# The value products of a GLA and a differential attention as three rounded passes in place of plain float32 products

## The reference

```
# GLA, per head; computed here as one causal 256x256 score matrix a head
attn = where(causal, q_dec @ k_inv.T, 0)
o = attn @ v + (carried state part)        # the value product
o = rms_norm(o, head_gain) * silu(r)
# differential attention, per head
p = softmax(q @ k.T + alibi bias), two of them
a = p[0] - lam * p[1]
o = a @ v                                  # the value product
o = rms_norm(o, head_gain) * (1 - lambda_init)
```

## Time and profile before

| | us |
|---|---|
| median of 3 runs | 2195.97 (2195.87 to 2196.18) |
| span of the profiled execution | 2193.8 |
| time around the span (median less span) | 2.2 |
| PE busy | 2188.1 (100% of the span) |
| DVE busy | 1242.7 (57%) |
| ACT busy | 1058.2 (48%) |
| mean granted TensorE clock | 1.000 of full |

### The profile page before, as it was taken

The page is one execution under the profiler, slowest core; times in us unless marked ns, Lnnn a source line. Parts: engine busy times, 40 slices in busy tenths (PEclk is TensorE's granted clock), DMA queues, the critical chain, the costliest instruction groups (busy, mean ns, idle before and its releaser), DMA issues.

```text
span 2193.8 us, 27239 instructions
## 1 busy us (share of the span) xinstructions
PE 2188.1 (100%) x9720; PEld 1808.9 (82%) x9720; DVE 1242.7 (57%) x1460; ACT 1058.2 (48%) x1428; POOL 283.0 (13%) x563
## 2 busy tenths in 40 slices
PE   9999999999999999999999999999999999999999
PEld 7888788888888888888888888888888888888887
DVE  5665566655555555555566676665555555555443
ACT  6666455444444444444456665554444444444333
POOL 3210334100000000001125333341000000000000
PEclk9999999999999999999999999999999999999999
DMA  8765667666666666666667666676666666666664
GB/s 264 210 189 176 189 202 218 203 215 203 203 202 213 201 202 206 200 205 203 201 202 217 196 207 202 204 223 210 199 207 200 215 200 203 205 210 194 195 193 163
DMA packets 252675, 447.01 MB, mean 204 GB/s; under 512 B 27665, under 2 KB 41969, under 8 KB 252593
## 3 DMA queue, kind: packets, MB, share of 16 engines
q1 hardware_dynamic: 236176, 428.79, 62.2%
q0 software_dynamic: 16240, 17.07, 2.7%
q10 hardware_dynamic: 176, 0.07, 0.0%
HBM read 414.37 MB, written 2.10 MB: 190 GB/s over the span
## 4 chain that ended last, share of the span: by engine, by line
PE 100%; DVE 0%; ACT 0%; issue 0%; POOL 0%; DVEq 0%; ACTq 0%; POOLq 0%
PE acc L641 32%; PE acc L639 32%; PE acc L640 32%; PE acc L651 1%; PE acc L656 0%; PE side L884 0%; PE tps L678 0%; PE side L727 0%; PE side L703 0%; PE side L762 0%; PE side L882 0%; PE side L898 0%; PE side L899 0%; PE side L900 0%; PE side L782 0%; PE side L780 0%
## 5 line engine op out<-in xcount | busy, mean ns | idle before, releaser
L1311 DVE TENSOR_TENSOR w_lo<-raw,w_hi 128x1024 fp32r<-128x1024 f32 x784 | 954.8, 1222 | 835.6 <-ACT w_hi L945 831.3
L945 ACT ACTIVATE w_hi<-raw 128x1024 fp32r<-128x1024 f32 x784 | 827.8, 1059 | 1002.9 <-PE acc L641 994.0
L639 PE MATMUL acc<-w_hi,xT 128*128 128x512 f32 x2016 | 787.6, 391 | 0.0
L641 PE MATMUL acc<-w_hi,xT 128*128 128x512 f32 x2016 | 784.4, 389 | 0.0
L640 PE MATMUL acc<-w_lo,xT 128*128 128x512 f32 x2016 | 784.4, 389 | 0.0
L639 PEld LDWEIGHTS acc<-w_hi,xT 128*128 128x128 f32 x2016 | 378.4, 188 | 79.0 <-issue 0.7
L640 PEld LDWEIGHTS acc<-w_lo,xT 128*128 128x128 f32 x2016 | 378.4, 188 | 78.9 <-issue 0.7
L641 PEld LDWEIGHTS acc<-w_hi,xT 128*128 128x128 f32 x2016 | 378.4, 188 | 78.9
L639 PE MATMUL acc<-w_hi,hT 128*128 128x512 f32 x700 | 272.3, 389 | 0.0
L640 PE MATMUL acc<-w_lo,hT 128*128 128x512 f32 x700 | 272.3, 389 | 0.0
L641 PE MATMUL acc<-w_hi,hT 128*128 128x512 f32 x700 | 272.3, 389 | 0.0
(11 more groups left out here) (204 smaller groups left out, 1372.2 us busy)
## 6 DMA issues: line engine op xcount, KB each, us to landing
raw<-in_ffn_w_in SPq DMA_DIRECT2D x352, 512.0 KB, 3.8
raw<-in_ffn_w_out SPq DMA_DIRECT2D x176, 512.0 KB, 4.7
raw<-in_gla_w_in SPq DMA_DIRECT2D x96, 512.0 KB, 4.3
raw<-in_w_kv SPq DMA_DIRECT2D x64, 512.0 KB, 4.6
raw<-in_gla_w_out SPq DMA_DIRECT2D x32, 512.0 KB, 4.9
raw<-in_diff_w_q SPq DMA_DIRECT2D x32, 512.0 KB, 4.6
raw<-in_diff_w_out SPq DMA_DIRECT2D x32, 512.0 KB, 4.9
tok<-scratch SPq DMA_DIRECT2D x352, 32.0 KB, 2.9
```

Source lines behind the costliest of these rows:

```text
L639: nc.tensor.matmul(acc[p][tb][:, :], hi, w_hi[:, slot, j, :], start=(kt + j == 0), stop=False)
L641: last = nc.tensor.matmul(acc[p][tb][:, :], lo, w_hi[:, slot, j, :], start=False, stop=(kt + j == n_kt - 1))
L945: nc.scalar.activation(w_hi[:, slot, :, :], raw[:, slot, :, :], ACT.Copy).then_inc(hi_done, 1)
L1311: nc.vector.tensor_tensor(w_lo[:, slot, :, :], raw[:, slot, :, :], w_hi[:, slot, :, :].bitcast(F32), ALU.subtract).then_inc(lo_done, 1)
```

## The change

Both value products are computed from operands that are split into a rounded high part and the rest, and each product is three float32r passes (high by high, high by low, low by high). For that:

- PE: `three` issues the passes. A GLA head has 9 matmuls of 512 columns in place of 3, a pair of differential heads 18 of 256 columns in place of 6.
- Values: ACT writes the rounded copy at the same place as before (`v_out`), and DVE then makes the low part from PSUM (`v_low_out`). `evacuated`, on which PE waits, is now raised by DVE.
- GLA scores: ACT rounds them (`scores_high`, (b, 3) of blocks 5 to 8), DVE makes the low part (`scores_low`, (b, 4)).
- Probabilities: ACT's copy now rounds; DVE makes the low part (`probs_low`, at (b, 2) of blocks 8 to 11). PE and SP wait for this (`p_low_done`) where they waited for ACT (`p_out`).
- The value buffers are single, not double, and three landing places of other turns are moved.

The diff, cut to its core:

```diff
@@ SP, move_probs
                 if k == 0:
                     sp.wait_ge(p_squared, n + 1)
                     if n:
-                        sp.wait_ge(p_out, 2 * n)
+                        sp.wait_ge(p_low_done, 2 * n)
@@ PE
+            def three(out_, at_hi, at_lo, v_hi, v_lo, start, stop):
+                nc.tensor.matmul(out_, at_hi, v_hi, start=start, stop=False)
+                nc.tensor.matmul(out_, at_hi, v_lo, start=False, stop=False)
+                return nc.tensor.matmul(out_, at_lo, v_hi, start=False, stop=stop)
             def gla_output(h):
                 pe.wait_ge(evacuated[h % 2], evac_count("gla_in", 8 + h))
                 if h == 0:
-                    pe.wait_ge(at_free, H_G)
+                    pe.wait_ge(at_lo_done, H_G)
...
-                nc.tensor.matmul(side[0][:, :], g_at[:, h, 0, :], g_v[:, h % 2, 0, :], start=True, stop=True)
-                nc.tensor.matmul(side[1][:, :], g_at[:, h, 1, :], g_v[:, h % 2, 1, :], start=True, stop=False)
-                nc.tensor.matmul(side[1][:, :], g_at[:, h, 2, :], g_v[:, h % 2, 0, :], start=False, stop=True).then_inc(o_done, 1)
+                for c, tb, start, stop in ((0, 0, True, True), (1, 1, True, False), (2, 0, False, True)):
+                    last = three(side[min(c, 1)][:, :], at_high[:, h, c, :], at_low[:, h, c, :], v_high[:, tb, :], v_low[:, tb, :],
+                                 start, stop)
+                last.then_inc(o_done, 1)
@@ PE, diff_output
-                pe.wait_ge(p_out, 2 * (n + 1))
+                pe.wait_ge(p_low_done, 2 * (n + 1))
...
@@ ACT
+            def v_out(phase, b, dst):
+                act.wait_ge(unit_used, block_end(phase, b))
+                for tb in range(TB):
+                    nc.scalar.activation(dst[:, tb, :], acc[b % 2][tb][:, :], ACT.Copy, scale=rstd[:, tb:tb + 1]).then_inc(v_hi_done, 1)
+            def scores_high(h):
+                act.wait_ge(at_free, h + 1)
+                nc.scalar.activation(at_high[:, h, :, :], g_at[:, h, :, :], ACT.Copy).then_inc(at_hi_done, 1)
@@ DVE
+            def scores_low(h):
+                dve.wait_ge(at_hi_done, h + 1)
+                nc.vector.tensor_tensor(at_low[:, h, :, :], g_at[:, h, :, :], at_high[:, h, :, :].bitcast(F32),
+                                        ALU.subtract).then_inc(at_lo_done, 1)
+            def v_low_out(n, b, high, low):
+                for tb in range(TB):
+                    dve.wait_ge(v_hi_done, TB * n + tb + 1)
+                    nc.vector.scalar_tensor_tensor(low[:, tb, :], acc[b % 2][tb][:, :], rstd[:, tb:tb + 1],
+                                                   high[:, tb, :].bitcast(F32), ALU.mult, ALU.subtract).then_inc(evacuated[b % 2], 1)
+                    if 9 <= b and k == 0:
+                        v_low_out(b - 9, b - 1, v_high, v_low)
+            def probs_low(n):
+                for half in range(2):
+                    dve.wait_ge(p_out, 2 * n + half + 1)
+                    nc.vector.tensor_tensor(d_at_low[:, n, 0:3, half, :]...
+                    if 9 <= b and k == (1 if b == 9 else 0):
+                        v_low_out(H_G + b - 9, b - 1, dv_high, dv_low)
+                    if 8 <= b and k == 2:
+                        probs_low(b - 8)
```

More of the change, by code:

```diff
@@ L237, in trunk @@
             g_r = sb("g_r", [P, TB, DV], F32, s1)
[L238 to L244, removed]
-            lam_rows = sb("lam_rows", [P, 4, HD], F32, s1)
+            lam_rows = sb("lam_rows", [P, 4, HD], F32, s1)
+            with ExitStack() as s2:
+                g_v = sb("g_v", [P, 2, TB, HV], F32, s2)
+            v_parts = sb("v_parts", [P, 2, TB, HV], F32R, s1)
+            with ExitStack() as s2:
+                a_raw = sb("a_raw", [P, KT, RANK], F32, s2)
+                a_w = sb("a_w", [P, KT, GATE_ROWS], F32R, s2)
+                a_T = sb("a_T", [GATE_ROWS, S], F32R, s2)
+                a_full = sb("a_full", [GATE_ROWS, S], F32, s2)
+                gate_raw = sb("gate_raw", [GATE_ROWS, DK], F32, s2)
+                w_gate = sb("w_gate", [GATE_ROWS, DK], F32R, s2)
+                gate_end = nc.sbuf_base
+            at_high = sb("at_high", [P, H_G, 3, P], F32R, s1)
+            at_low = sb("at_low", [P, H_G, 3, P], F32R, s1)
+            o_turned = sb("o_turned", [P, TB, CB], F32, s1)
+            sb("gap_gate", [P, (gate_end - nc.sbuf_base) // 4], F32, s1)
             with ExitStack() as s2:
@@ L265, in trunk @@
             d_q = sb("d_q", [P, 2 * H_D, S], F32, s1)
[L266 to L268 removed]
+            with ExitStack() as s2:
+                d_k = sb("d_k", [P, 2 * H_D, S], F32, s2)
+                d_v = sb("d_v", [P, 2, TB, CB], F32, s2)
+            d_at_low = sb("d_at_low", [P, H_D // 2, 4, 2, P], F32R, s1)
+            dv_parts = sb("dv_parts", [P, 2, TB, CB], F32R, s1)
+            d_at = sb("d_at", [P, H_D, 3, P], F32R, s1)
             probs = sb("probs", [P, 2, 3 * P], F32, s1)
@@ L894, in diff_output @@
                     pe.wait_ge(o_tok, H_G + n)
-                pe.wait_ge(p_out, 2 * (n + 1))
+                pe.wait_ge(p_low_done, 2 * (n + 1))
                 for e in range(2):
                     h, cols = 2 * n + e, slice(e * S, (e + 1) * S)
-                    nc.tensor.matmul(side[0][:, cols], d_at[:, h, 2, :], d_v[:, n % 2, 0, cols], start=True, stop=True)
-                    nc.tensor.matmul(side[1][:, cols], d_at[:, h, 0, :], d_v[:, n % 2, 0, cols], start=True, stop=False)
-                    last = nc.tensor.matmul(side[1][:, cols], d_at[:, h, 1, :], d_v[:, n % 2, 1, cols], start=False, stop=True)
+                    for c, tb, out_, start, stop in ((2, 0, side[0], True, True), (0, 0, side[1], True, False),
+                                                     (1, 1, side[1], False, True)):
+                        last = three(out_[:, cols], d_at[:, h, c, :], d_at_low[:, n, c, e, :], dv_high[:, tb, cols],
+                                     dv_low[:, tb, cols], start, stop)
                 last.then_inc(o_done, 1)
@@ L1106, in _ @@
                         decays(2 * (b - 4) + (k == 6))
+                    if 5 <= b < 9 and k == 3:
+                        scores_high(b - 5)
                     if 9 <= b and k == 2:
@@ L1506, in _ @@
                         scores_out(b - 5)
+                    if 9 <= b and k == 0:
+                        v_low_out(b - 9, b - 1, v_high, v_low)
+                    if 5 <= b < 9 and k == 4:
+                        scores_low(b - 5)
                     if 10 <= b and k == 3:
```

32 lines of the change are left out of this document (24 added, 8 removed).

## The result

| | median us | from to | runs |
|---|---|---|---|
| before | 2196.18 | 2195.87 to 2196.22 | 5 |
| after | 2207.74 | 2206.82 to 2209.55 | 5 |

The ratio is 1.0056, with a 95% interval of 1.0045 to 1.0066: the change makes the kernel 11.6 us slower. The forecast was 2204.3, its range 2199.5 to 2209.5. The profiled execution of after took 2206.82 with a span of 2204.9, 11.1 more than the span before.

The account below looks back on a forecast made before the run. PE bounds the kernel, by its own instruction stream and every moment it must wait. Passes -3.9, six waits +8.7 and blocks 8 and 9 +3.5 sum to +8.3 on 2195.97: 2204.3 us, range 2199.5 to 2209.5.

Parts of the forecast that it names:

- The passes: At the value products on PE, float32r passes shorter than float32: 0.54 per GLA, 0.44 per differential product, together -3.9 us.
- The slow end of that term: At the value products, the three passes are paced like float32 and gain nothing; near 2209 us, chance 0.03.
- The six waits: At four GLA and the last two differential products, PE idles 1.45 each for DVE's values' low part: +8.7 us.
- Blocks 8 and 9: In the differential phase, DVE's added work and a late load make PE late by (9, 7): +3.5 us, bounds 0 to 5.
- Steps 1 and 2: At (8, 2) `probs_low` delays softmax 4 by 0.97; SP's moves go 4.1 later, load (9, 1) lands late, softmax 5 2.1 late.
- Step 3: ACT's turned heads shift from 1311.41 to 1313.5, so PE waits 1.9 at `scores(6)`.
- Step 5: At (9, 7) PE starts 3.5 later than 1328.12, the 1.9 at `scores(6)` contained in that.
- The rival of the clock: Waits of 1.5 or more put the following unit at the lower clock, seven times 2.72: +19, 2223 us, chance 0.02.
- The rival of late loads: SP's later wait starves ACT, DVE and PE at the starts of blocks 9, 10, 11, about 2 each: 2210 us, chance 0.10.
- The sign: Slower, chance 0.86; the passes win if PE idles under 0.65 at each of six products and blocks 8 and 9 stay hidden.
- the chain hidden: In blocks 8 and 9 DVE's added work costs PE nothing while the six waits remain: +4.8, 2200.8 us, chance 0.15.

Follow-up runs that it names:

- values_early: The changed kernel with seven of eight value copies and low parts moved ahead of the last unit's split on ACT and DVE; 2196.20 us, ratio 1.0000 to before.
- gla_only: The changed kernel with the differential value products left in float32 as before, so only GLA products run as three passes; 2199.33 us, ratio 1.0014 to before.
- sp_late: The kernel before with only SP's wait ahead of the small moves released later, by DVE's low part of a unit; 2208.67 us, ratio 1.0055.
- moves_later: The changed kernel with SP's small moves behind the load of (b, 0) instead of ahead of it; 2202.41 us, ratio 1.0028 to before.

## Why the prediction was right, and where it was off

- **The passes** were right to 0.1: 2.04 for nine and 2.16 for eighteen, -4.0 in all. `values_early` shows the gain bare. The slow end of that term, a rival at 0.03, is out.
- **The six waits** cost 1.36 where I had 1.45, at five places, with the order and the releaser as written. `gla_only` and `values_early` show it by leaving them in alone and taking them out. At the sixth, (11, 1), the step failed that reads "the same wait of SP is moved by about 5 us at (10, 0) and (11, 0) ... I cost it at nothing, with 0.5 if the cover is short". The wait was moved by 5 as said (first move at 1351.85, less the 7 by which after is behind there, against 1339.76), but I took ACT's three units of lead for the cover, and the value copy has none: it stands directly behind the split that waits for the late load. That is 4.0 of delay in place of 1.45, of which 1.3 is low clock and 1.3 the late load. `sp_late` shows the late load without any low part: 0.9. `values_early` takes the copy out from behind the split, and the loss goes with the loads still late.
- **Blocks 8 and 9**: +4.4 where I had +3.5. Steps 1 and 2 held up to SP (1.01 for `probs_low` against 0.97; SP's first move at 1294.80 on the clock of before against 1294.8; the load's issue at 1299.07 against 1299.1). The load then took 5.87 to ACT's start, where my bounds were 4.6 and 5.2 (the trace of before had warned: its loads issued between small moves at 1347.84 and 1350.30 landed 6.0 and 5.8 later), so softmax 5 was 3.0 late and not 2.1. Step 3 is thus 2.7 and not 1.9. Step 5 put the rest of the wait at (9, 7); it was all paid at `scores(6)`, and by the time of (9, 7) DVE was no longer late against PE: softmax 6 starts at 1323.88, on PE's new clock, 7.54 behind, 0.1 earlier than before. `moves_later` shows the two apart: 0.7 and 1.5 of delay when the load is in time.
- **The rival of the clock** was wrong for the pauses that it named and right about two that I had not weighed. I had weighed it for pauses of 1.5, by the 2.2 of idle PE in the first 25 us, and for all of them together. The pauses at the value products of this length (1.07 by the matmul's row) leave the clock alone in all these traces; so the 0.02 for seven falls was fair. But the earlier trace rows was weak evidence: one execution of `gla_only` shows a fall in those very 25 us, behind 1.63. And my own forecast had a pause of 1.9 with 1.6 behind it, and "late loads" named longer ones; for these I priced the pause alone. That is the term the sum lacks: 1.7 at `scores(6)` and 1.3 at (11, 1), 3.0 together, where the span grew by 2.8 more than the 8.3 of the forecast. The late load at (11, 1) adds another 1.3, and the six waits of 1.36 and a pause in blocks 8 and 9 of 2.7 where I had 3.5 take the same off. That these cancel is luck.
- **The rival of late loads** (2210, chance 0.10) had the right mechanism at two of its three places, the starts of blocks 9 and 11, though not at 10. What came is a mixture of it and the forecast, and lies between their two times. `sp_late` shows that such loads alone can cost PE 0.9 at (11, 1), under the 2 that the rival had.
- **The sign** was decided as said: idle time under 0.65 per product, with the chain hidden, would have made the passes win. With both moved, no value product behind its block waits any more, and the kernel is 1.7 faster than before, though the interval just includes no change; with the low part of the probabilities off DVE it is 3.0 faster, and the interval leaves no change out.

What isn't settled is why the same pause brings the clock down in one execution and not in another: of the twelve pauses in these profiles before which the matmul's row shows 2.2 to 4.3 of idle time, ten were followed by a fall, and the two without were the same place in two executions of one kernel. Nor do the traces say where between 1.3 and 2.2 falls begin: the only pause there, 1.63 at the start of `gla_only`, was followed by one.

## What to carry to other kernels

When a product gets a second operand from a second engine, look at what stands in front of that instruction in its engine's program, not at how busy the engine is. A split for three units on can wait, the value that PE needs next can't; exchanging the two was worth 11.5 us here and made no unit late for PE. When a wait of the queue that issues loads is moved to a later releaser, follow every load behind it to the first instruction without lead, and put the moves behind the load where they need not be ahead. And a pause of TensorE of over 2 us should be priced at 1.5 to 1.8 times itself, by the starts of the matmuls: that is what such a pause cost here where the clock fell.

## What the runs showed of the hardware

- After TensorE had idled 1.1 to 1.3 us by the matmul's row the granted clock stayed 1.00 (four GLA products, the last product, two made pauses, and (9, 7) of `moves_later`). After 2.2 to 4.3 us it was 0.50 to 0.60 in the first window of 2 us behind, near the lower level of 1.2 GHz, with PE busy, in ten of twelve cases. Where worked out from the starts, that cost 1.3 to 2.8 each. After 1.63 at the start of one `gla_only` execution it was 0.50.
- A float32r pass of 512 columns starts 0.227 behind the last, one of 256 columns 0.12, with new weights for each; at the low clock they take 0.43 and 0.21. Three such passes of 512 columns, 0.68, are cheaper than one float32 matmul, 0.86.
- A load of 512 KB took 4.6 us from issue to landing in the median of this phase, but loads issued between small moves took longer: 5.8 and 6.0 to landing in the kernel before (at 1350.30 and 1347.84), 4.9 to 5.9 from issue to the split that waited for them in the changed kernel (seven loads), and 6.4 for one in `sp_late`.
- A DVE subtraction of 128x1024 took 1.71 in place of 1.22 beside a GpSimd subtraction that took 2.42 in place of 1.98.
